# Tail of a two-block transformer kernel: who scales the first two row tiles, a split last product, and the order of bank additions

## What is computed

```
merged = (sigmoid(g_diff) * (o_diff @ w_proj_diff[layer])
          + sigmoid(g_mla) * (o_mla @ w_proj_mla[layer]))
x = x + merged @ w_out[layer]
...
return rms_norm(x, norm_final)      # x * rsqrt(mean(x*x) + eps) * gain, by row
```

## Time and profile before

| what | us |
|---|---|
| median of 3 runs | 1083.74 |
| lowest, highest | 1083.55, 1084.2 |
| the profiled execution's own time | 1083.35 |
| its span in the profile | 1081.6 |
| TensorE busy | 1066.9 (99%) |
| VectorE busy | 747.4 (69%) |
| ScalarE busy | 430.8 (40%) |

### The profile page before, as it was taken

The page is one execution under the profiler, slowest core; times in us unless marked ns, Lnnn a source line. Parts: engine busy times, 40 slices in busy tenths (PEclk is TensorE's granted clock), DMA queues, the critical chain, the costliest instruction groups (busy, mean ns, idle before and its releaser), DMA issues.

```text
span 1081.6 us, 13616 instructions
## 1 busy us (share of the span) xinstructions
PE 1066.9 (99%) x5373; PEld 856.3 (79%) x5373; DVE 747.4 (69%) x1182; ACT 430.8 (40%) x670; POOL 0.2 (0%) x4
## 2 busy tenths in 40 slices
PE   9999999999999999999999999999999999999997
PEld 6777877877878888888888887887776776888886
DVE  7998877868668887854488744655568536464498
ACT  7513655343442223222222234654357543232254
POOL 0000000000000000000000000000000000000000
PEclk9999999999999999999999999999999999999999
DMA  8422122121213323233422135333120322033212
GB/s 283 123 78 79 48 70 79 67 91 39 79 50 116 117 78 107 59 88 110 144 78 88 49 98 156 78 117 117 44 78 3 115 78 78 1 117 117 95 42 78
DMA packets 100239, 95.59 MB, mean 88 GB/s; under 512 B 5952, under 2 KB 91216, under 8 KB 100176
## 3 DMA queue, kind: packets, MB, share of 16 engines
q1 hardware_dynamic: 100000, 94.71, 27.8%
q10 hardware_dynamic: 176, 0.02, 0.0%
HBM read 92.60 MB, written 2.10 MB: 88 GB/s over the span
## 4 chain that ended last, share of the span: by engine, by line
PE 86%; DVE 8%; ACT 3%; issue 2%; DMA 1%; DVEq 0%; ACTq 0%
PE ring L1136 22%; PE ring L1138 22%; PE ring L1137 22%; DVE w_lo L2064 2%; PE bank L1136 2%; PE bank L1138 2%; PE bank L1137 2%; PE bank L1600 1%; PE bank L1395 1%; PE bank L1367 1%; PE bank L1300 1%; PE bank L1380 1%; PE bank L1624 1%; PE bank L1573 1%; PE ring L1463 1%
## 5 line engine op out<-in xcount | busy, mean ns | idle before, releaser
L1136 PE MATMUL ring<-act_hi,w_hi 128*128 128x512 f32 (+2 forms) x808 | 320.2, 396 | 0.9 <-DVE xT L2447 0.5
L1138 PE MATMUL ring<-act_hi,w_lo 128*128 128x512 f32 (+2 forms) x808 | 313.5, 388 | 0.0
L1137 PE MATMUL ring<-act_lo,w_hi 128*128 128x512 f32 (+2 forms) x808 | 313.2, 388 | 0.0
L1702 ACT ACTIVATE w_hi<-w_raw 128x2048 fp32r<-128x2048 f32 (+5 forms) x95 | 157.9, 1663 | 252.7 <-PE ring L1138 195.9
L2064 DVE TENSOR_TENSOR w_lo<-w_raw,w_hi 128x2048 fp32r<-128x2048 f32 (+4 forms) x100 | 188.0, 1882 | 4.0 <-ACT w_hi L1702 3.8
L1136 PEld LDWEIGHTS ring<-act_hi,w_hi 128*128 128x128 f32 x808 | 151.8, 188 | 37.1 <-issue 3.9
L1137 PEld LDWEIGHTS ring<-act_lo,w_hi 128*128 128x128 f32 x808 | 151.9, 188 | 31.4 <-issue 1.9
L1138 PEld LDWEIGHTS ring<-act_hi,w_lo 128*128 128x128 f32 x808 | 151.7, 188 | 31.4
L1136 PE MATMUL ring<-hidH,w_hi 128*128 128x512 f32 x176 | 68.5, 389 | 0.0
L1137 PE MATMUL ring<-hidL,w_hi 128*128 128x512 f32 x176 | 68.5, 389 | 0.0
L1138 PE MATMUL ring<-hidH,w_lo 128*128 128x512 f32 x176 | 68.5, 389 | 0.0
(11 more groups left out here) (417 smaller groups left out, 1659.1 us busy)
## 6 DMA issues: line engine op xcount, KB each, us to landing
w_raw<-in_w_in SPq DMA_DIRECT2D x30, 1024.0 KB, 5.3
w_raw<-in_w_up SPq DMA_DIRECT2D x22, 1024.0 KB, 5.1
w_raw<-in_w_out SPq DMA_DIRECT2D x6, 1024.0 KB, 5.3
w_raw<-in_w_down SPq DMA_DIRECT2D x8, 768.0 KB, 4.6
w_raw<-in_w_down SPq DMA_DIRECT2D x8, 640.0 KB, 4.3
w_raw<-in_w_in SPq DMA_DIRECT2D x7, 512.0 KB, 4.8
xin<-in_xt SPq DMA_DIRECT2D x8, 256.0 KB, 3.9
xT<-in_xt SPq DMA_DIRECT2D x2, 1024.0 KB, 6.5
```

The costliest lines, as they stand in the source:

```text
L1136: pe.matmul(out, ah, bh, start=(first and n == 0), stop=False)
L1137: pe.matmul(out, ah, bl, start=False, stop=False)
L1138: mm = pe.matmul(out, al, bh, start=False, stop=(last and n == len(pairs) - 1))
L1702: return act.activation(out, src, func, **more)
```

## The change

It makes three edits.

1. Rows 0 and 1: ScalarE no longer scales the early half, and VectorE no longer multiplies it by the gain beforehand. VectorE scales both halves by factor and gain, in two SCALAR_TENSOR_TENSORs a row, and the two rows' final stages stand ahead of the addition of bank (6, 0). SP sends each of the two rows as one transfer of 512 KB.
2. The last product (6, 1) is computed in two column halves of 256 into two banks (bank 1, and bank 2 for the second half), each with its own addition. ScalarE squares row 3's late half in two parts; VectorE adds the first part's share to the mean with one more TENSOR_SCALAR.
3. v_sum stands ahead of c_sum 4 in the list. TensorE waits for c_sum >= 3, which then implies both readers of bank 2, before it writes the second half of product (6, 1) there.

```diff
--- before.py
+++ after.py
@@ -863,15 +863,15 @@
         both("prod", 4)
         split_form("T4")
         both("u_sum")
+        both("v_sum")
         both("c_sum", 4)
-        both("v_sum")
         each("sq_early", 2, 3)
         both("prod", 5)
         both("c_sum", 5)
-        each("scaled", 0, 1, 2, 3)
+        each("scaled", 2, 3)
         both("prod", 6)
+        each("final", 0, 1)
         stage("c_sum", 6, 0)
-        each("final", 0, 1)
         stage("c_sum", 6, 1)
         each("final", 2, 3)
 
@@ -947,6 +947,10 @@
         RES_OF = {2: (0, 0), 5: (1, 0), 6: (0, 256)}
         ROWS_OF = {2: (0, 0), 4: (2, 1), 5: (0, 1), 6: (2, 0)}
 
+        def column_cuts(n, t):
+
+            return [slice(0, 256), slice(256, 512)] if (n, t) == (6, 1) else [slice(0, 512)]
+
         def left_of(n):
 
             if n in S_OF:
@@ -955,7 +959,6 @@
             return [m[:, 4 * half:4 * half + 4, at:at + 256] for m in (mH, mL)]
 
         EARLY_ROWS, LAST_ROWS = (0, 1, 2, 3), (0, 1, 2, 3)
-        SCALED_ROWS = tuple(s[1] for s in order if s[0] == "scaled")
 
         def raw_of(c):
 
@@ -1110,12 +1113,16 @@
             quarter_in(b21, 1, 0, block_in[1])
             sp.wait_ge(tile_done, upto(("pm", KD - 1)))
             sp.dma_start(gfin[:], g_fin_d.partition_broadcast(P)).then_inc(con_in, 16)
-            for n, b in enumerate(LAST_ROWS):
-                for half, made in ((early_half[b], out_act), (1 - early_half[b], out_dve)):
+            rows = out_d.rearrange("(b p) d -> p b d", p=P)
+            for b in (0, 1):
+                sp.wait_ge(out_dve, 2 * b + 2)
+                sp.dma_start(rows[:, b, :], xo[:, b, :]).then_inc(out_done, 16)
+            for b in (2, 3):
+                for half, made, count in ((1, out_act, b - 1), (0, out_dve, b + 3)):
                     at = slice(512 * half, 512 * half + 512)
-                    sp.wait_ge(made, n + 1)
-                    sp.dma_start(out_d.rearrange("(b p) d -> p b d", p=P)[:, b, at], xo[:, b, at]).then_inc(out_done, 16)
-            sp.wait_ge(out_done, 32 * NB)
+                    sp.wait_ge(made, count)
+                    sp.dma_start(rows[:, b, at], xo[:, b, at]).then_inc(out_done, 16)
+            sp.wait_ge(out_done, 16 * 6)
 
 
         @block.tensor
@@ -1659,15 +1666,19 @@
                         pe.wait_ge(part_sum, 2 * t + 4)
                     to = bank[2 * (n % 3) + t]
                     opened = n in RES_OF
-                    if opened:
-                        half, b0 = RES_OF[n]
-                        for j in range(4):
-                            pe.matmul(to[:, P * j:P * j + P], xT[:, 4 * half + j, b0 + P * t:b0 + P * t + P], ident,
-                                      start=(j == 0), stop=False, is_transpose=True)
                     lh, ll = left_of(n)
                     wh, wl = weights(PROD[n])
-                    product(to[:], [((lh[:, k, at], ll[:, k, at]), (wh[:, k, :], wl[:, k, :])) for k in range(4)],
-                            first=not opened).then_inc(prod_mm, 1)
+                    for cut in column_cuts(n, t):
+                        if cut.start == 256:
+                            pe.wait_ge(c_sum, 3)
+                            to = bank[2]
+                        if opened:
+                            half, b0 = RES_OF[n]
+                            for j in range(cut.start // P, cut.stop // P):
+                                pe.matmul(to[:, P * j:P * j + P], xT[:, 4 * half + j, b0 + P * t:b0 + P * t + P], ident,
+                                          start=(P * j == cut.start), stop=False, is_transpose=True)
+                        product(to[:, cut], [((lh[:, k, at], ll[:, k, at]), (wh[:, k, cut], wl[:, k, cut])) for k in range(4)],
+                                first=not opened).then_inc(prod_mm, 1)
                 elif kind == "res":
                     b = 2 + s[1]
                     out = open_bank(s)
@@ -2027,18 +2038,25 @@
                     act.wait_ge(c_sum, k + 1)
                     if k >= 2:
                         act.wait_ge(ssf_ready, k - 1)
-                    A(mt[k % 2][:], xo[:, b, 512 * half:512 * half + 512], ACT.Square,
-                      accum_out=ssf[:, 2 * b + half:2 * b + half + 1]).then_inc(ssf_ready, 1)
+                    if (kind, b) == ("final", 3):
+                        A(mt[k % 2][:, 0:256], xo[:, b, 0:256], ACT.Square, accum_out=ssf[:, 8:9]).then_inc(ssf_ready, 1)
+                        act.wait_ge(c_sum, k + 2)
+                        A(mt[k % 2][:, 256:512], xo[:, b, 256:512], ACT.Square,
+                          accum_out=ssf[:, 2 * b + half:2 * b + half + 1]).then_inc(ssf_ready, 1)
+                    else:
+                        A(mt[k % 2][:], xo[:, b, 512 * half:512 * half + 512], ACT.Square,
+                          accum_out=ssf[:, 2 * b + half:2 * b + half + 1]).then_inc(ssf_ready, 1)
                     if kind == "final":
                         first = 512 * early_half[b]
-                        act.wait_ge(f_var, EARLY_ROWS.index(b) + 1)
-                        act.wait_ge(ssf_ready, k + 1)
+                        act.wait_ge(f_var, EARLY_ROWS.index(b) + 1 + (b == 3))
+                        act.wait_ge(ssf_ready, k + 1 + (b == 3))
                         A(rsf[:, b:b + 1], ssf[:, 2 * b + half:2 * b + half + 1], ACT.Ln, bias=sst[:, b:b + 1], scale=1.0 / D).then_inc(act_step, 1)
                         act.wait_ge(act_step, step())
                         A(rsf[:, b:b + 1], rsf[:, b:b + 1], ACT.Exp, scale=-0.5).then_inc(f_rs, 1)
-                        act.wait_ge(f_rs, LAST_ROWS.index(b) + 1)
-                        act.wait_ge(xo_g, SCALED_ROWS.index(b) + 1)
-                        A(xo[:, b, first:first + 512], xo[:, b, first:first + 512], ACT.Identity, scale=rsf[:, b:b + 1]).then_inc(out_act, 1)
+                        if b >= 2:
+                            act.wait_ge(f_rs, b + 1)
+                            act.wait_ge(xo_g, b - 1)
+                            A(xo[:, b, first:first + 512], xo[:, b, first:first + 512], ACT.Identity, scale=rsf[:, b:b + 1]).then_inc(out_act, 1)
 
 
         @block.vector
@@ -2763,10 +2781,11 @@
                     n, t = s[1:]
                     b, half = ROWS_OF[n][0] + t, ROWS_OF[n][1]
                     to = xo[:, b, 512 * half:512 * half + 512]
-                    dve.wait_ge(prod_mm, 2 * n + t + 1)
                     if n == 5:
                         dve.wait_ge(part_sum, 7 + t)
-                    TT(to, xo[:, t, 512:1024] if n == 2 else to, bank[2 * (n % 3) + t][:], ALU.add).then_inc(c_sum, 1)
+                    for i, cut in enumerate(column_cuts(n, t)):
+                        dve.wait_ge(prod_mm, 2 * n + t + 1 + i)
+                        TT(to[:, cut], (xo[:, t, 512:1024] if n == 2 else to)[:, cut], bank[2 if cut.start == 256 else 2 * (n % 3) + t][:, cut], ALU.add).then_inc(c_sum, 1)
                 elif kind == "scaled":
                     b = s[1]
                     k, half = EARLY_ROWS.index(b), early_half[b]
@@ -2782,7 +2801,14 @@
                 elif kind == "final":
                     b = s[1]
                     at = slice(512 * (1 - early_half[b]), 512 * (1 - early_half[b]) + 512)
-                    dve.wait_ge(f_rs, LAST_ROWS.index(b) + 1)
+                    if b == 3:
+                        dve.wait_ge(f_var, 4)
+                        dve.wait_ge(ssf_ready, NB + 4)
+                        TS(sst[:, 3:4], ssf[:, 8:9], 1.0 / D, sst[:, 3:4], ALU.mult, ALU.add).then_inc(f_var, 1)
+                    dve.wait_ge(f_rs, b + 1)
+                    if b < 2:
+                        dve.wait_ge(con_in, 48)
+                        STT(xo[:, b, 0:512], xo[:, b, 0:512], rsf[:, b:b + 1], gfin[:, 0:512], ALU.mult, ALU.mult).then_inc(out_dve, 1)
                     STT(xo[:, b, at], xo[:, b, at], rsf[:, b:b + 1], gfin[:, at], ALU.mult, ALU.mult).then_inc(out_dve, 1)
```

## The result

| | median us | lowest to highest | runs |
|---|---|---|---|
| before | 1083.91 | 1083.34 to 1084.91 | 13 |
| after | 1086.23 | 1085.82 to 1086.55 | 13 |

The ratio is 1.002, with a 95% interval of 1.0012 to 1.0028. The change costs 2.3 us where 2.1 were forecast, and 1086.23 lies in the range of 1084.9 to 1086.8. The interval lies above 1, so the kernel did get slower. By the medians that is 0.21%, a hair outside the bound of 0.2% that I had put the forecast just inside of; on which side of that bound it would fall was a toss-up, as the chances of 0.52 and 0.45 said.

The account below looks back on a forecast made before the run. TensorE's matmuls fill 99% of the span; in the tail ScalarE sets the end, VectorE right behind. 1.90 us (stall and moved scalings) plus 0.20 (split's extra) gave +2.1, put at 1085.8 us, range 1084.9 to 1086.8.

Parts of the forecast that it names:

- stall: VectorE waits at rows 2 and 3's early means for ScalarE's squares, so block 5's additions start 0.84 us later.
- split's extra: ScalarE, row 3's late square: two half-width ACTIVATEs take 0.83 us instead of 0.63, adding 0.20.
- Part 1: Bank additions swapped, v_sum ahead of c_sum 4: a new VectorE stall of 0.84 us before block 5's additions.
- Part 2: Rows 0 and 1 scaled on VectorE alone: row 2's last addition 1.46 us later in the queue, 0.40 absorbed.
- slack: Row 2's square already waited 0.40 us after its addition because ScalarE was busy; that much delay is absorbed.
- Part 3: Last tile in two column halves: +0.20 us on ScalarE; TensorE's later end costs nothing, as nobody waits.
- Part 4: Output DMAs, rows 0 and 1 as one transfer each: 0 us, 3.13 us kept behind the last scaling.
- Rival A: ScalarE's tail: its relief decides, faster or level; 1083.6 us, at best a gain of 1.0 to 1082.7; chance 0.05.
- Rival B: VectorE's early means: not held, so no stall; 0.84 us goes, +1.3 is left, 1085.0 us; chance 0.07.
- Rival C: ScalarE's row 3: half squares don't overlap the accumulator read; 0.19 us more, +2.3, 1086.1 us; chance 0.10.
- Rival D: TensorE's last product: short matmuls become the bound; at a 0.28 us step +2.7, 1086.4 us; chance 0.03.

Follow-up runs that it names:

- no_split: The change with the last tile whole, one square for row 3 and no extra mean; median 1085.92 us, 0.31 below the change.
- both_moves_whole: The change with row 2's addition ahead of rows 0 and 1's scalings, early squares and means behind block 5's additions, last tile whole; 1083.86 us against 1084.27 before.
- filled: As both_moves_whole, but the last bank's addition between row 1's two scalings and row 2's first transfer ahead of row 1's; 1083.92 us against 1084.27 before.
- swap_alone: The kernel before with only v_sum moved ahead of c_sum 4 in the list; median 1084.87 us, 0.60 above before.
- add_first: The change with row 2's last addition moved ahead of the scalings of rows 0 and 1; median 1084.79 us, 1.44 below the change.
- both_moves: The same reordering as both_moves_whole, but with the last tile in column halves as in the change; 1083.79 us against 1083.97 before.

## Why the prediction was right, point by point

The tail against the steps of the prediction, each counted from the start of u_sum's last addition:

| step | predicted | measured |
|---|---|---|
| block 5's additions start (stall) | 4.07 | 4.09 |
| row 2's last addition starts | 9.13 | 9.14 |
| row 2's square starts | 9.85 | 9.86 |
| split's extra | 0.20 | 0.20 (no_split), 0.18 (alone) |
| last scaling starts | 13.42 | 13.41 |
| last scaling's end to span's end | 3.13 | 3.05 |
| TensorE's end, later than whole | 0.4 | 0.1 |

Part 1: +0.84 predicted, 0.86 shown by undoing it and by making it alone. Part 2: 1.46 of the queue less 0.40 of slack, 1.06; alone it is 1.07, undone 1.08. Part 3 on ScalarE: 0.20. Part 4: nothing, shown only as the end of 3.05 us.

Rival A (ScalarE's relief decides) was wrong for the order that the change has. In both_moves_whole the relief shortens the tail by 0.3, since VectorE reaches the last addition just as late; in filled, where that addition comes at TensorE's end, the tail is 0.9 shorter, nearly the 1.0 that the rival put at best, of which the medians show 0.35 (an interval that holds no change). Rival B fell with swap_alone. Rival C, that the halves' squares would not overlap, fell by the row at 1079.46: the accumulator's read lies under the next square, and the step is 0.40, less than my 0.414. From its first square's start to Ln, row 3 takes 0.98 (1079.16 to 1080.14), against 0.80 with one square (no_split, 1078.77 to 1079.57). The two widths that my 0.20 was worked out from the earlier trace rows read a PSUM bank; the squares read xo, and their durations, 0.62 and 0.40, differ by as much. The Trainium skill ("ScalarE: Activation LUTs", rules for kernel authors) gives its fixed 0.3 us for an ACTIVATE with a bias as a pointer operand, which these squares do not have; taken for them, it would have made 0.3 of the 0.20. Its slope holds (0.22 us for 256 columns), but its figure is a duration, and the queue gives up less: the square behind a scaling of 0.72 us starts 0.63 after it (1071.75 to 1072.38 before). Rival D: TensorE's short step stayed at 0.12 in every run with the halves, and nobody waited for it.

The extra mean of row 3 was hidden, as forecast, but with 0.18 us to spare (done at 1079.96, Ln at 1080.14) and not 0.35; in add_first and both_moves it is not hidden.

What was off is small. TensorE's end was overpriced by 0.3 us: I counted the halves from 1071.67, as if four transposes still stood ahead of the first matmul; two do, and it starts 0.13 behind them (1072.19 to 1072.32) instead of 0.35. I also counted 24 steps and the last one's whole duration, which is one step of 0.12 too many. It cost nothing either way. And the time grew by 2.3, not 2.1. Tail and end together explain 2.04; in the twelve experiments the difference of the medians strays from that of tail and end by -0.26 to +0.33, so the remaining 0.28 is of the size of that scatter. I do not claim a cause for it. What carries the prediction is that the steps on the path came out within 0.02 us. The medians, which stray by 0.3, could not have shown it so closely.

## What to carry to other kernels

When two engines are both full in a tail, relieving the one that ends the chain is worth only the slack of the other. Ask first what the moved work now stands in front of: here four scalings that nobody waited for stood ahead of one addition that ScalarE did wait for, and reordering alone took back 1.5 of the 2.1 us. Exchanging equal operations is not free if the instruction right behind waits, through another engine, for the one that became second. And a tail that is shortened can release its output in a lump: read the transfers' share over the last microseconds before counting the gain.

## What the runs showed that I had not expected

When the tail was 0.9 us shorter, 0.45 of it came back behind the last scaling, with the transfer engines full: 377 to 412 GB/s at a share of 0.96 to 1.05 until 1080, one stretch longer than before (375, 385 and 350 GB/s from 1076 to 1079, then 266). The kernels in between were already close to that: in both_moves_whole, with a tail 0.3 shorter, the engines are as full from 1077 to 1081 (393, 389, 381 and 367 GB/s), and the end is still 3.10. A TensorE product in two halves of 256 columns with its own opening each ended only 0.1 us later than the whole one (3.45 us from its transposes' start at 1072.19, against 3.36), less than the 0.4 that I had added up. And ScalarE's square of 256 columns, read included, takes 0.40 us of its queue, against 0.63 for 512.
